# In-projection of a hybrid decoder layer: the slab of gate columns moved to second place, and the convolution's second gate slab computed by seven products of halves

## What is computed

```python
def hybrid_mixer(h, w_in, ...):
    points = [int(p) for p in np.cumsum(IN_SPLITS)[:-1]]
    (q, k_c, v_c, k_s, v_s, k_w, v_w, g_nsa, mq, mk, mv, mo, mi, mf, cu) = jnp.split(h @ w_in, points, axis=-1)
    a_out = nsa_attention(q, k_c, v_c, k_s, v_s, k_w, v_w, g_nsa, ...)
    ...
    qk = jax.nn.silu(causal_depthwise_conv(jnp.concatenate([mq, mk], axis=-1), mlstm_conv_w, mlstm_conv_b))
    hm = mlstm_chunkwise(mq.reshape(shp), mk.reshape(shp), mv.reshape(shp), mi + mlstm_i_bias, mf + mlstm_f_bias)
    ...
    ca, cg = jnp.split(cu, 2, axis=-1)
    c = causal_depthwise_conv(ca * jax.nn.sigmoid(cg), conv_w, conv_b)
    c = jax.nn.silu(layernorm(c, conv_ln_g, conv_ln_b))
    return jnp.concatenate([a_out, hm, c], axis=-1) @ w_out
```

## Time and profile before

| what | value |
|---|---|
| time, median of 3 runs | 1425.89 us (1425.21 to 1428.28) |
| time of the profiled execution | 1428.03 us |
| its span in the trace | 1426.2 us |
| granted clock of PE, mean over the span | 0.943 of full speed |
| PE busy | 1205.7 us, 85% of the span |
| DVE busy | 483.6 us, 34% |
| ACT busy | 255.3 us, 18% |
| chain that ended last | PE 52%, DMA 43% of the span |
| memory traffic | 479.34 MB, mean 336 GB/s |

### The profile page before, as it was taken

How to read it: one execution, slowest core, us unless ns; L and a number is a source line. 1 busy time by engine, 2 the same in 40 slices (tenths; PEclk the granted TensorE clock), 3 DMA queues, 4 the chain that set the end, 5 groups by cost and what they waited for, 6 DMA issues and landing times.

```text
span 1426.2 us, 17903 instructions
## 1 busy us (share of the span) xinstructions
PE 1205.7 (85%) x7431; PEld 708.9 (50%) x7431; DVE 483.6 (34%) x1001; ACT 255.3 (18%) x629; POOL 13.5 (1%) x82
## 2 busy tenths in 40 slices
PE   8999999999999998669689958768587695876977
PEld 7999999766568753123244314224142241422422
DVE  5398997663875431121110220111101111011123
ACT  2101111444600122011111101002020010201112
POOL 2000000000010000000000000000000000000000
PEclk9999999999999999889999989989899898998989
DMA  9958677431644899999999999999999999999995
GB/s 318 274 158 194 167 161 236 119 82 38 165 112 166 346 413 426 429 427 427 428 428 428 426 428 427 427 427 429 428 426 427 429 427 425 431 426 426 429 427 237
DMA packets 133362, 479.34 MB, mean 336 GB/s; under 512 B 47804, under 2 KB 105632, under 8 KB 107552
## 3 DMA queue, kind: packets, MB, share of 16 engines
q1 hardware_dynamic: 126816, 477.58, 85.9%
q10 hardware_dynamic: 6464, 0.58, 0.4%
HBM read 476.05 MB, written 2.10 MB: 335 GB/s over the span
## 4 chain that ended last, share of the span: by engine, by line
PE 52%; DMA 43%; ACTq 2%; DVE 1%; ACT 1%; issue 1%; DVEq 0%
DMA ring<-in_expert_w_up_dram 36%; PE PS L1127 13%; PE PS L1447 10%; DMA spare<-in_expert_w_up_dram 6%; PE PS L1269 5%; PE PS L1169 3%; PE PS L1434 3%; PE PS L1246 2%; PE PS L1638 2%; ACTq L1862 2%; PE PS L1425 1%; PE PS L1221 1%; PE PS L1119 1%; PE PS L1648 1%; PE PS L1188 1%; PE PS L1509 1%
## 5 line engine op out<-in xcount | busy, mean ns | idle before, releaser
L1447 PE MATMUL PS<-ring,XG 128*32 128x512 f32 x1296 | 222.2, 734 | 147.9 <-DMA ring<-in_expert_w_up_dram 107.3
L1447 PEld LDWEIGHTS PS<-ring,XG 128*32 128x32 f32 x1296 | 57.6, 131 | 274.9 <-issue 271.8
L3068 DVE TENSOR_TENSOR hTe<-PS,sg 128x128 f32<-128x128 f32 (+1 forms) x31 | 9.9, 320 | 349.3 <-ACT sg L2193 349.1
L2885 DVE TENSOR_TENSOR x<-PS,x 128x1024 f32<-128x1024 f32 x41 | 50.2, 1225 | 209.8 <-PE PS L1526 208.4
L2181 ACT ACTIVATE Hs<-PS 128x512 f32<-128x512 f32 x30 | 17.9, 597 | 463.1 <-PE PS L1447 349.8
L1434 PE MATMUL PS<-ring,XG 128*64 128x512 f32 x192 | 84.6, 594 | 18.0 <-DMA ring<-in_expert_w_up_dram 14.5
L1526 PE MATMUL PS<-Y,SW 128*128 128x512 f32 (+2 forms) x176 | 90.6, 627 | 1.5 <-ACT ro L2289 1.5
L1447 PE MATMUL PS<-spare,XG 128*32 128x512 f32 x208 | 66.0, 793 | 27.8 <-DMA ring<-in_expert_w_up_dram 27.8
L1436 PE MATMUL PS<-ring,XG 128*64 128x512 f32 x192 | 85.0, 595 | 0.0
L1425 PEld LDWEIGHTS PS<-sel,xn 128*128 128x128 f32 x640 | 75.3, 191 | 13.0 <-issue 12.7
L1425 PE MATMUL PS<-sel,xn 128*128 128x128 f32 x640 | 77.6, 280 | 1.4 <-DVE x L2885 1.4
(11 more groups left out here) (494 smaller groups left out, 1577.2 us busy)
## 6 DMA issues: line engine op xcount, KB each, us to landing
ring<-in_expert_w_up_dram SPq DMA_DIRECT2D x53, 2048.0 KB, 23.8
ring<-in_expert_w_gate_dram SPq DMA_DIRECT2D x53, 2048.0 KB, 26.9
ring<-in_expert_w_down_dram SPq DMA_DIRECT2D x51, 2048.0 KB, 27.1
ring<-in_w_in_dram SPq DMA_DIRECT2D x17, 2048.0 KB, 9.5
spare<-in_expert_w_gate_dram SPq DMA_DIRECT2D x9, 2048.0 KB, 26.2
spare<-in_expert_w_up_dram SPq DMA_DIRECT2D x8, 2048.0 KB, 23.9
spare<-in_expert_w_down_dram SPq DMA_DIRECT2D x8, 2048.0 KB, 27.3
ring<-in_w_in_dram SPq DMA_DIRECT2D x16, 512.0 KB, 7.3
```

Of the source, the lines that this page charges most:

```text
L1447: mm = pe.matmul(PS[r:r + 32, 0, :], gathered_rows(q, 4 * c + j)[:, column:column + 32], weight_rows(slots[u], 4 * (c % 2) + j), start=(c ...
L2885: dve.tensor_tensor(y, new, old, ALU.add).then_inc(sc_added, 1)
```

## The change

"small" goes from ninth to second place in `SLABS`, so the other gate slab of the convolution, "cg1", comes third, and "cg1" joins `FAST_SLABS`: its two units are no longer done by `project` but by `fast_products`. The numbers in the code that depend on the order follow.

```diff
-SLABS = ["cg0", "cg1", "ca0", "ca1", "mq0", "mq1", "mk0", "mk1", "small", "kc0", "vc0", "ks0", "kw0",
+SLABS = ["cg0", "small", "cg1", "ca0", "ca1", "mq0", "mq1", "mk0", "mk1", "kc0", "vc0", "ks0", "kw0",
...
-            units += [(n, part, "columns", s, 0), (n - 1, "small", "folded", 0, 0), (n, part, "columns", s, 1)]
+            units += [(n, part, "columns", s, 0), (n, "small", "folded", 0, 0), (n, part, "columns", s, 1)]
...
-FAST_SLABS = ("ca0", "ca1", "mq0", "mq1", "mk0", "mk1", "vc0", "ks0", "kw0", "vs0", "q0", "q1", "q2", "q3", "vw0")
+FAST_SLABS = ("cg1", "ca0", "ca1", "mq0", "mq1", "mk0", "mk1", "vc0", "ks0", "kw0", "vs0", "q0", "q1", "q2", "q3", "vw0")
...
-BETWEEN_ACT = {after("small", 2): ["forget_logs"], after("vc", 1): ["conv_silu"], after("vs", 1): ["decays"],
+BETWEEN_ACT = {units_with("small") - 1: ["forget_logs"], after("vc", 1): ["conv_silu"], after("vs", 1): ["decays"],
...
-                if u == 3:
+                if u == 2:
                     turn_params()
...
             follow(0)
             follow(1)
+            follow(2)
...
             conv_taps(0, 3)
-            follow(2)
+            follow(3)
             conv_taps(3, 6)
-            follow(3)
+            follow(4)
```

More of the change, by code:

```diff
@@ L2473, in _ @@
             conv_taps(0, 3)
-            follow(2)
+            follow(3)
             conv_taps(3, 6)
-            follow(3)
+            follow(4)
             conv_taps(6, 9)
-            follow(4)
+            follow(5)
             conv_taps(9, 12)
-            finish(5)
+            finish(6)
             conv_taps(12, 13)
@@ L2509, in _ @@
             key_taps(3, ML_TAPS)
-            left_sums(6)
-            right_sum(6)
-            last_sum(6)
+            left_sums(7)
+            right_sum(7)
+            last_sum(7)
             conv_taps(13, 18)
-            follow(6)
+            follow(7)
             dve.wait_ge(forget_step, 5)
@@ L2528, in _ @@
             conv_taps(18, 20)
-            follow(7)
+            follow(8)
             dve.wait_ge(mconv_step, 8 * ML_TAPS)
@@ L2546, in _ @@
                     ins.then_inc(blk_ready, 1)
-            follow(8)
+            follow(9)
             dve.wait_ge(g_spread, 1)
@@ L2560, in _ @@
             conv_taps(20, 21)
-            follow(9)
+            follow(10)
             conv_taps(21, 25)
-            follow(10)
+            follow(11)
             for h in range(ML_H):
@@ L2578, in _ @@
             dve.reciprocal(ml[:, 7, :, :], ml[:, 6, :, :]).then_inc(den_ready, 1)
[L2579 to L2582, removed]
+            keep_m1(12)
+            left_sums(13)
+            combine(12)
+            right_sum(13)
             conv_taps(25, 28)
-            last_sum(12)
+            last_sum(13)
             conv_taps(28, TAPS)
-            follow(12)
+            follow(13)
             dve.wait_ge(conv_step, TAPS * CT)
@@ L2591, in _ @@
             dve.tensor_tensor(tmp, cacc, cacc, ALU.mult).then_inc(ln_step, 1)
-            follow(13)
+            follow(14)
             dve.wait_ge(ln_step, 4)
@@ L2595, in _ @@
             dve.tensor_tensor(cacc, cacc, pT[:, 0:1, 0:T].broadcast_to([P, CT, T]), ALU.mult).then_inc(ln_step, 1)
-            finish(14)
+            finish(15)
             mo_v = mo[:, :, :].rearrange("p t (h d) -> p t h d", h=ML_H)
```

## The result

The changed kernel takes 1438.19 us (median of 6 runs, 1437.34 to 1439.18), the kernel before beside it 1426.75 us (6 runs). The ratio is 1.0079, 95% interval 1.0067 to 1.0091: slower by 11.3 us (9.6 to 13.0). The prediction was 1436.0 us, 1432 to 1440.

A forecast was written before the change was run, and what follows sets the result against it. PE was taken to bound the kernel (85% busy, chain without a gap from 41.35 us). Idle 10.51 + clock 1.5 - 1.28 - 0.66 = +10.07 us on the 1425.89 us median: 1436.0 us, 8-in-10 range 1432.0 to 1440.0.

The forecast's parts named there:

- The place and the cause: Before the first fast slab: plain "cg1" (13.81 us) hides ACT's DMA issues; fast "cg1" must wait for unit 0's save.
- The idle time: PE ahead of "cg1": ready at 30.47 us, stands still 10.51 us until ACT saves unit 0 at 40.98 us.
- rival B: ACT's issues before its first save: held up 4.6 us more behind "small"'s packets, giving 1440.6 us; chance 0.08.
- The clock: PE after the wait: restart at half clock costs 1.5 us, with 0 and 3.4 us as the ends.
- The savings: PE up to "kc0": seven products for "cg1" save 1.28 us, the vanished wait ahead of "ca0" 0.66 us.
- rival A: ACT's issues beside "small"'s packets: ACT free some 9.5 us sooner, PE hardly stops, 1.94 us gained, 1423.9 us; chance 0.06.
- DMA and DVE at no cost: Early slabs: "cg1" landing about 5 us later costs nothing; DVE's extra 6.5 us of work costs 0 to 0.3 us.
- All of it reaches the end: From "kc0" to the end: PE's shift delays the expert loads and the end by the full 10.07 us.
- rival C: Between 265 and 554 us: loss partly taken back where PE waits for other engines, 1427 to 1432 us; chance 0.04.

The follow-up runs named there:

- experiment 1: Changed kernel with ACT's eight router DMA issues moved behind its save of "small", from ahead of its first save: 1425.35 us, ratio 0.9985.
- experiment 4: Changed kernel with the old `SLABS` (seven products for "cg1" without the move of "small"), parameters turned behind unit 1: 1428.04 us, ratio 1.0009.
- experiment 8: Changed kernel and plain-"cg1" variant ("small" second) rerun on one chip, each also with unread products in PE's wait: 1438.87, 1436.18, 1430.27, 1430.70 us.
- experiment 3: Kernel before with "small" second but "cg1" still in the plain manner: 1430.32 us, ratio 1.0021.
- experiment 6: Changed kernel with only the last four of ACT's eight router DMA issues moved behind its save of "small": 1430.36 us, ratio 1.0032.

## Why the prediction was right

**The place and the cause: right.** The prediction said that plain "cg1" lies beside ACT's issues and hides them, and that the fast one would wait for unit 0. The PE row shows it, and experiment 1 removes the wait without touching what the change did and gets back 13 us of "kc0". (The trace has 25 issues ahead of the first save from 16 us on, not 24; no sum uses the count.)

**The idle time: 10.51 us predicted, 10.20 measured** in the profile and 11.18 in the second one. Start of "cg1": 40.98 predicted, 40.89 and 42.84 measured. ACT's last issue is not as fixed as I took it. In the eight profiles with the early "small" and all issues in place it was free between 38.97 and 40.93 us, 39.96 in the mean; with "small" at its old place at 39.07 (before) and 39.67 (experiment 4). Some of rival B, well under 1 us, may be in this; with two profiles on the other side it is not shown.

**The clock: right in kind, in size too small for one profile and right for the other.** I took 1.5 us from restarts with 2.3 to 3.4 us at half clock. In the first profile half clock lasted 5.6 us after the restart, and seven fast slabs took 90.45 - 7 x 12.53 = 2.7 us too long. In the second one they took 89.33 - 7 x 12.53 = 1.6 us too long, after 3.2 us at half clock. In the first profile this term is what moved "kc0" from the predicted 130.2 to 131.2 us.

**The savings: right.** Taken as 1.28 + 0.66 us. In experiment 1 "kc0" is 2.0 us sooner, and the time 0.15% (0.06 to 0.24%) lower: that is rival A's outcome of 1.94 us, reached by another road.

**DMA and DVE at no cost: right.** From 14 to 20 us SP's queue passes 4378 packets and ACT's 35, "small" among them:

```profile
q1 hardware_dynamic: 4378, 1.13, 109.6%
q10 hardware_dynamic: 35, 0.01, 0.8%
```

So "small" met almost none of ACT's packets, and rival A had nothing to work with. Its premise, that ACT's issues go no faster than 281 packets per us, doesn't hold in general either: in experiment 1 three issues of 512 rows took 0.64 to 0.66 us each. The slab more kept DVE busy 6.2 us longer (489.8 against 483.6 us), 6.5 predicted. DVE begins "cg1"'s sums at 32.46 us without a wait. Its wait of 2.86 us for the gates is gone:

```profile
140.11 0.16 DVE L2502 TENSOR_TENSOR gates<-gates,fi_b 128x16 f32<-128x16 f32 x1
```

**All of it reaches the end: right within what can be told.** "kc0" is 11.0 us late, the first long wait for experts 10.9 us, the end by the ratio 11.3 us (9.6 to 13.0). So rival C took nothing that these figures could show; for the plain pair of experiment 8 something like it stays open.

**The number.** 1436.0 against 1438.19: 0.9 us is the kernel before, 1426.75 in these runs and 1425.89 in those shown, and the rest is 1.3 us. By the change alone it is 10.07 us against 11.3 (9.6 to 13.0), so the rest is within the noise; the clock's term, 2.7 and 1.6 us in the two profiles where I took 1.5, would give a part of it.

## What to carry to other kernels

An engine's first useful work can be held up by DMA issues that stand ahead of it in its program; as long as a slower piece of work on another engine covers them they cost nothing, and speeding up or moving that piece lays them bare. Before a piece is put forward, ask for every wait of the new first step which engine counts that semaphore up, and what stands ahead of it there. Here the change was worth 0.15% once the eight issues stood behind the first saves, and cost 0.8% without that.

## What the runs showed of the hardware that was not expected

PE's granted clock fell around waits as short as 3.3 us: in experiment 3 (3.29 us) before the wait ended, in experiment 6 (3.28 us) and in the plain kernel of experiment 8 (3.85 us) only 0.5 and 0.3 us after the restart, when PE was at work again. After the restarts it was at half for 3 to 6 us. With products that nobody reads in the wait, and 1.0 to 1.3 us of it left, it stayed full in four profiles.

Eight issues of 512 short rows each held ACT for 14 us, from 24.7 to 38.9 us, 1.8 us each. The size of an issue alone doesn't set this: where ACT had issued nothing for some us before, the first three of the same eight took 0.64 to 0.66 us each (experiment 1), while SP's queue was as full. What slows the later ones was not isolated.
